# GpSimd's preparation in a two-layer encoder trunk: input matrices ahead of the angle tables, and the first transposes of h one product later

## The chip, the cores and the metric

The kernel runs on one core of one Trainium2 chip. The metric is device time in microseconds (us), the median of repeated executions. Engines go by these names: TensorE (PE; its weight loads are PEld), VectorE (DVE), ScalarE (ACT), GpSimd (POOL) and SyncE (SP).

## What is computed

Two layers over 256 tokens of 1024 channels, all in float32. Each layer is a feed-forward stage (FFN 1), a mixer, and a second feed-forward stage (FFN 2), each with a residual and a layer norm:

```
x <- LN(alpha*x + 0.5*SwiGLU_1(x))
x <- LN(alpha*x + HybridMixer(x))
x <- LN(alpha*x + 0.5*SwiGLU_2(x))

def swiglu_ffn(x, w_up, w_down):            # w_up 1024 x 5632, w_down 2816 x 1024
    gate, up = jnp.split(x @ w_up, 2, axis=-1)
    return (jax.nn.silu(gate) * up) @ w_down

# ssm_branch, 32 groups of 16 channels, 64 complex states each
    a_bar = jnp.exp(lam * dt)
    b_bar = ((a_bar - 1.0) / lam)[:, :, None] * lax.complex(b_re, b_im)
    bu = einsum(u, b_bar)
    states = associative_scan(a_seq, bu)
    y = einsum(states, c_mat).real + d_skip * u
```

The mixer has a state-space branch (above), and a branch of sparse attention with an additive position bias. The state-space branch needs, per layer, matrices that depend on the weights alone: `b_bar`, a product of the output matrix with powers of `a_bar`, and tables of cosine and sine of the angles that turn the scan into a real one. The change is about when GpSimd makes these.

## The kernel before, in words

**The main stream.** TensorE multiplies in float32 by splitting each operand in a high part (rounded to the matmul's format) and a low part, the rest: three matmuls for each product (lines 744 to 746). SyncE loads weight tiles of 128 x 1024 into a ring of four buffers (`raw`, loads at line 329). ScalarE writes the high part into `whi` (`split_hi`, line 430), VectorE the low part into `wlo` (`split_lo`, line 1246); both are rings of eight. A tile's load waits until the tile four before it is split; a split waits until TensorE has used the tile eight before it.

**An FFN** has 11 chunks of 256 hidden channels. `up_chunk` takes the four weight tiles of a chunk twice, once for each half t of the tokens (t = 0, 1), 24 matmuls of 512 columns each (`up_pass`). ScalarE then makes `silu` (line 453), VectorE the product h (line 1274), and TensorE transposes h (`h_transpose`, line 768) for the down product, which ScalarE and VectorE again split (lines 444 and 1264). Chunks 0 to 2 are written out (`PEEL`), the other eight are a hardware loop. In FFN 1 of layer 0 (f = 0) chunk 0 and 1 are written out in `opening`. Then come 22 tiles of the down product. After its tiles 2, 6, 11 and in the last part, TensorE does a quarter of the state-space preparation (`prepare_quarter`, lines 923 to 929): it transposes the four 128 x 128 matrices of `b_bar`, which ScalarE copies to `b_t` (line 468), and multiplies `b_bar` with `c_t`.

**The order in `silu` and h.** On ScalarE and on VectorE the four splits for the chunk two ahead stand between the silu (or h) of t = 0 and that of t = 1. An engine runs its instructions in program order.

**GpSimd** runs `prepare(l)`: for layer 0 during FFN 1 of layer 0, for layer 1 during FFN 2 of layer 0. In order:

- transfers of the parameters (line 1696) and of a column `d_col`; for layer 0 the table of attention biases (`gather_bias`, line 1681, 31 small operations, and its store);
- a wait for VectorE's `clamp` (line 1355), which stands behind chunk 0's h; then the angles, whose sine and cosine ScalarE takes (line 464, behind chunk 1);
- squares, powers and quotients of 128 x 16 (`small`), transfers of the raw input and output matrices `b_raw` and `c_t`, 512 KB each (lines 1752, 1753);
- the tables `tab_c`, `tab_s` by doubling, 7 steps with up to 128 x 512 elements, with `b_bar` as scratch. Between two steps the factor is squared, and copied by two multiplications by one;
- for each quarter q of four: `prepare_b(q)`, 12 operations of 128 x 128, then 6 for `c_t`. There is one `b_bar` buffer, so that `prepare_b(q + 1)` waits until TensorE has used quarter q.

Nearly all of these go through one helper (line 1647), and each waits for the one before it.

```
            def prepare_b(q):
                js = slice(4 * q, 4 * q + 4)
                if q > 0:
                    pool.wait_ge(S["bt_done"], NQ * l + q)
                    pool.wait_ge(S["k0_done"], NQ * l + q)
```

VectorE flips the sign of half of `c_t` (`negate_c`, line 1361) behind the first split of the down product. It needs `c_t` to have landed, and GpSimd's products of `c_t` need it.

Of the kernel before, what the change touches and what calls it, by code (L numbers as in the profile page):

```python
# [13 lines left out]
P = 128  # L14
# [87 lines left out]
def build(nc, A, out):  # L102
# [19 lines left out]
    b_t = sb("b_t", [P, 4, NQ, P])  # L122
# [45 lines left out]
    b_bar = place("b_bar", [P, 4, P])  # L168
# [151 lines left out]
    with block:  # L320
# [102 lines left out]
        def _(act):  # L423
# [23 lines left out]
            def up_chunk(i, f, s, c, b, first=False):  # L447
                for t in range(NT):
# [6 lines left out]
                    if t == 0:  # L455
                        for q in range(4):
                            split_hi(i, s + RING + q)
# [8 lines left out]
            def prepare_b(l, q):  # L466
                act.wait_ge(S["bt_done"], NQ * l + q + 1)
                nc.scalar.copy(b_t[:, :, q, :], ps[:, 0, :].rearrange("p (v n) -> p v n", v=4)
                               ).then_inc(S["bt_ready"], 1)
# [271 lines left out]
        def _(pe):  # L741
# [51 lines left out]
            def up_chunk(i, f, s, c, b):  # L793
                for t in range(NT):
                    up_pass(i, f, s, c, b, t)

            def opening():
# [45 lines left out]
                h_transpose(0, 0, 0, False)  # L843
# [68 lines left out]
            def prepare_quarter(l, f, q):  # L912
# [9 lines left out]
                for v in range(4):  # L922
                    ins = nc.tensor.transpose(ps[:, 0, v * P:v * P + P], b_bar[:, v, :], ident[:, :])
                ins.then_inc(S["bt_done"], 1)
                for r in range(4):
                    o = ps[32 * r:32 * r + 32, 1, 256:288]
                    j = 4 * q + r
                    nc.tensor.matmul(o, b_bar[:, 0, 32 * r:32 * r + 32], c_t[:, 0, j, :], start=True, stop=False)
                    ins = nc.tensor.matmul(o, b_bar[:, 1, 32 * r:32 * r + 32], c_t[:, 1, j, :],
# [3 lines left out]
            def ffn(f, stage, s0, following, prep):  # L933
# [4 lines left out]
                for c in range(2, PEEL):  # L938
                    up_chunk(0, f, s0 + 4 * c, c, c % 2)
# [31 lines left out]
            def ssm_in(l, half):  # L971
# [7 lines left out]
                for q in (2 * half, 2 * half + 1):  # L979
                    u = u_t[:, q, :].rearrange("p (c e) -> p c e", e=2)  # L980
                    for v in range(2):
                        at = (q % 2) * SEQ + v * HALF
                        for e in range(2):
                            for r in range(4):
                                rows = slice(32 * r, 32 * r + 32)
                                ins = nc.tensor.matmul(ps[:, BU + r, at:at + HALF],  # L986
                                                       b_t[rows, 2 + v if e == 0 else v, q, :], u[rows, :, e],
# [241 lines left out]
        def _(dve):  # L1229
# [37 lines left out]
            def up_chunk(i, f, s, c, b, first=False, early=False):  # L1267
                for t in range(NT):
# [8 lines left out]
                    if t == 0:  # L1277
# [93 lines left out]
            def ffn(f, s0, prep):  # L1371
                for c in range(PEEL):
                    up_chunk(0, f, s0 + 4 * c, c, c % 2, first=c == 0, early=c < 2)
                    if c == 0 and prep is not None:
                        clamp(prep)
# [3 lines left out]
                for k in range(HK - RING):  # L1379
# [3 lines left out]
                    if k == 0 and prep is not None:  # L1383
                        negate_c(prep)
# [253 lines left out]
        def _(pool):  # L1638
# [48 lines left out]
            def prepare(l):  # L1687
# [10 lines left out]
                if l == 0:  # L1698
                    gather_bias()
# [16 lines left out]
                op(m(5), m(4), k(12), ALU.add, S["angle_ready"])  # L1716
                pool.wait_ge(S["sincos_ready"], l + 1)
                si, co, mag = m(6), m(7), m(10)

# [32 lines left out]
                pool.dma_start(b_raw[:, :, :, :], A["ssm_b_rows"][l]).then_inc(S["b_landed"], 16)  # L1752
                pool.dma_start(c_t[:, 0:2, :, :], A["ssm_c_rows"][l]).then_inc(S["c_landed"], 16)

                n = 1
# [188 lines left out]
```

## Time and profile before

| what | value |
| --- | --- |
| median of three runs | 1118.56 us (1118.28 to 1119.14) |
| span of the profiled execution, first to last instruction | 1117.5 us |
| what the median has beyond that span | 1.06 us |
| busy: TensorE / its weight loads | 1105.8 us (99%) / 917.9 us (82%) |
| busy: VectorE / ScalarE / GpSimd | 752.0 us (67%) / 561.1 us (50%) / 391.1 us (35%) |
| DMA | 208.95 MB, mean 187 GB/s |

The profile is one execution, read out by hardware. For the profiled execution no time but its span is given; the runs' times include a little before the first and after the last instruction. A row of the order of time has: start in us, duration in us, engine, line, operation, output <- inputs, count, and in brackets the idle time of the engine before it and what ended it. TensorE's matmuls overlap: what counts is the distance from one start to the next, not the duration.

### The profile page before, as it was taken

Reading aid. Unit: us, or ns where it says so; the run is one execution under the profiler, and the core shown is the slowest. Engines: PE = TensorE matmul, PEld = TensorE weight load, DVE = VectorE, ACT = ScalarE, POOL = GpSimd, SP = SyncE. Lnnn points to the kernel's source line nnn. Section 1 sums busy time; section 2 is a strip of 40 time slices with the busy share of each in tenths; the row PEclk is TensorE's granted clock in tenths of the full one; section 3 lists DMA queues with packets and bytes.
Section 4 is the critical chain, followed back from the end, with each engine's and each line's share of the span. In section 5 each row is a group of like instructions: output and inputs, shape, how many; then the busy total and the mean of one; then the engine's idle time right before and its main releaser. Section 6 shows DMA issues by size and latency. Waiting matters only on the chain.

```text
span 1117.5 us, 17726 instructions
## 1 busy us (share of the span) xinstructions
PE 1105.8 (99%) x5979; PEld 917.9 (82%) x5979; DVE 752.0 (67%) x1073; ACT 561.1 (50%) x805; POOL 391.1 (35%) x560
## 2 busy tenths in 40 slices
PE   9999999999999999999999999999999999999997
PEld 7788888997788888888888888889877888888886
DVE  6657755789977865675575555467898787565544
ACT  6545433674873554543344544336748645453540
POOL 4889975107700188998500000011275000000001
PEclk9999999999999999999999999999999999999999
DMA  9776753644565577565367575536535666657541
GB/s 287 242 228 208 247 176 113 211 136 137 157 223 192 166 224 242 184 221 187 112 201 227 159 245 192 192 91 226 164 112 160 209 199 210 211 172 241 189 150 38
DMA packets 158655, 208.95 MB, mean 187 GB/s; under 512 B 12760, under 2 KB 107128, under 8 KB 158592
## 3 DMA queue, kind: packets, MB, share of 16 engines
q1 hardware_dynamic: 155232, 202.29, 56.7%
q10 hardware_dynamic: 2592, 3.67, 1.2%
q0 software_dynamic: 768, 2.17, 0.6%
q8 instruction: 37, 0.61, 0.2%
q14 instruction: 26, 0.21, 0.1%
HBM read 207.02 MB, written 1.06 MB: 186 GB/s over the span
## 4 chain that ended last, share of the span: by engine, by line
PE 82%; DVE 8%; ACT 3%; issue 3%; DMA 2%; SPq 1%; POOLq 0%; POOL 0%; DVEq 0%; ACTq 0%
PE ps L744 25%; PE ps L746 25%; PE ps L745 25%; DVE wlo L1246 4%; PE ps L768 2%; DMA raw<-in_ffn_w_up 1%; DVE score L1441 1%; ACT whi L430 1%; DMA raw<-in_w_in 1%; PE ps L758 1%; PE ps L986 1%; DVE gates L1413 1%; PE ps L1123 1%; PE ps L1125 1%; PE ps L1126 1%
## 5 line engine op out<-in xcount | busy, mean ns | idle before, releaser
L1246 DVE TENSOR_TENSOR wlo<-raw,whi 128x1024 fp32r<-128x1024 f32 (+1 forms) x371 | 475.7, 1298 | 188.4 <-ACT whi L430 174.2
L430 ACT CAST whi<-raw 128x1024 fp32r<-128x1024 f32 (+1 forms) x371 | 384.7, 1044 | 287.1 <-PE ps L746 225.2
L744 PE MATMUL ps<-whi,xh 128*128 128x512 f32 x976 | 384.4, 394 | 0.2 <-DVE wlo L1246 0.2
L746 PE MATMUL ps<-whi,xl 128*128 128x512 f32 x976 | 377.8, 387 | 0.0
L745 PE MATMUL ps<-wlo,xh 128*128 128x512 f32 x976 | 377.4, 387 | 0.0
L744 PEld LDWEIGHTS ps<-whi,xh 128*128 128x128 f32 x976 | 183.3, 188 | 39.0 <-issue 3.4
L746 PEld LDWEIGHTS ps<-whi,xl 128*128 128x128 f32 x976 | 183.2, 188 | 37.8
L745 PEld LDWEIGHTS ps<-wlo,xh 128*128 128x128 f32 x976 | 183.5, 188 | 34.9
L1671 POOL TENSOR_TENSOR rstd<-var_eps,cst 128x1 f32<-128x1 f32 x12 | 18.2, 1518 | 529.8 <-DVE var_eps L1295 520.7
L744 PE MATMUL ps<-whi,hh 128*128 128x512 f32 (+1 forms) x355 | 139.5, 393 | 0.0
L746 PE MATMUL ps<-whi,hl 128*128 128x512 f32 (+1 forms) x355 | 137.7, 388 | 0.0
L745 PE MATMUL ps<-wlo,hh 128*128 128x512 f32 (+1 forms) x355 | 137.6, 388 | 0.0
L1274 DVE SCALAR_TENSOR_TENSOR h<-silu,ps 128x256 f32<-128x256 f32 x88 | 36.4, 416 | 97.6 <-ACT silu L453 97.6
L453 ACT ACTIVATE silu<-ps 128x256 f32<-128x256 f32 x88 | 33.0, 379 | 134.9 <-PE ps L746 134.8
L746 PEld LDWEIGHTS ps<-whi,hl 128*128 128x128 f32 x355 | 66.7, 188 | 13.9
L744 PEld LDWEIGHTS ps<-whi,hh 128*128 128x128 f32 x355 | 66.7, 188 | 13.5
L745 PEld LDWEIGHTS ps<-wlo,hh 128*128 128x128 f32 x355 | 66.7, 188 | 13.1
L1840 POOL TENSOR_TENSOR h_st<-tab_c,gates 128x512 f32<-128x512 f32 x8 | 10.3, 1294 | 115.3 <-DVE wlo L1246 88.6
L1647 POOL TENSOR_TENSOR small<-small 128x16 f32<-128x16 f32 x102 | 38.2, 375 | 8.5 <-ACT small L464 0.7
L1123 PE MATMUL ps<-xh,whi 128*128 128x256 f32 x128 | 37.4, 292 | 0.0
L1125 PE MATMUL ps<-xl,whi 128*128 128x256 f32 x128 | 36.2, 283 | 0.0
L1126 PE MATMUL ps<-xh,wlo 128*128 128x256 f32 x128 | 36.1, 282 | 0.0
(195 smaller groups left out, 1209.3 us busy)
## 6 DMA issues: line engine op xcount, KB each, us to landing
raw<-in_ffn_w_up SPq DMA_DIRECT2D x351, 256.0 KB, 4.0
raw<-in_ffn_w_down SPq DMA_DIRECT2D x176, 256.0 KB, 3.1
raw<-in_w_in SPq DMA_DIRECT2D x128, 256.0 KB, 3.4
raw<-in_w_branch SPq DMA_DIRECT2D x32, 256.0 KB, 3.3
raw<-in_w_out SPq DMA_DIRECT2D x32, 256.0 KB, 3.8
bias_g<-bias_rows ACTq DMA_DIRECT2D x16, 192.0 KB, 3.7
raw<-in_w_in SPq DMA_DIRECT2D x16, 148.0 KB, 2.3
affine<-in_ln_g SPq DMA_DIRECT2D x4, 512.0 KB, 5.6
```

Source lines behind the costliest of these rows:

```text
L430: nc.scalar.copy(whi[:, s % RING, 0:w], raw[:, s % RAW, 0:w]).then_inc(S["hi_done"], 1)
L453: nc.scalar.activation(silu[:, t, :], ps[:, 2 * b + t, 0:CW], ACT.Silu).then_inc(S["silu_done"], 1)
L744: nc.tensor.matmul(o, ah, bh, start=start, stop=False)
L745: nc.tensor.matmul(o, ah, bl, start=False, stop=False)
L746: return nc.tensor.matmul(o, al, bh, start=False, stop=stop)
L768: ins = nc.tensor.transpose(ps[:, 4 + b, k * SEQ + i * P:k * SEQ + (i + 1) * P], h[:, b, i, k * P:(k + 1) * P], ident[:, :])
L1123: nc.tensor.matmul(o, hi, xh[:, k, :], start=k == 0 and m % 2 == 0, stop=False, skip_group_check=True)
L1125: nc.tensor.matmul(o, hi, xl[:, k, :], start=False, stop=False, skip_group_check=True)
L1126: ins = nc.tensor.matmul(o, lo, xh[:, k, :], start=False, stop=k == KT - 1, skip_group_check=True)
L1246: nc.vector.tensor_tensor(wlo[:, s % RING, 0:w], raw[:, s % RAW, 0:w], f32(whi[:, s % RING, 0:w]), ALU.subtract).then_inc(S["split_done"], 1)
L1274: nc.vector.scalar_tensor_tensor(out=h[:, b, t, :], in0=silu[:, t, :], scalar=0.5, in1=ps[:, 2 * b + t, CW:2 * CW], op0=ALU.mult, op1=ALU. ...
L1647: ins = nc.gpsimd.tensor_tensor(o, a, b, f)
```

## The change

It does five things.

1. GpSimd's order in `prepare`: the bias table runs after the angles, while ScalarE takes sine and cosine; the transfers of `b_raw` and `c_t` are issued ahead of it. After the powers come `prepare_b(0)`, `prepare_b(1)` and all four products of `c_t`, then the tables, then `prepare_b(2)` and `prepare_b(3)`.
2. `b_bar` has two buffers (q % 2), so that only quarters 2 and 3 wait for TensorE. The tables use the last quarter of `b_t` as scratch, and `b_t` is laid out quarter by quarter.
3. The copies by multiplication by one between table steps are gone: two pairs of `small` rows change places.
4. VectorE runs `clamp` ahead of chunk 0 and `negate_c` behind chunk 2. `clamp` waits for the parameters' landing.
5. In FFN 1 of layer 0, chunk 0, silu and h of t = 1 run ahead of the four splits on ScalarE and VectorE; and TensorE transposes chunk 0's h not ahead of chunk 2 but inside its first pass, after two of the four tiles.

```
-                    if t == 0:
+                    if t == (1 if f == 0 and first else 0):
                         for q in range(4):
                             split_hi(i, s + RING + q)
...
                 up_pass(0, 0, 4, 1, 1, 1, False)
-                h_transpose(0, 0, 0, False)
...
                 for c in range(2, PEEL):
-                    up_chunk(0, f, s0 + 4 * c, c, c % 2)
+                    first_turn = (lambda: h_transpose(0, 0, 0, False)) if f == 0 and c == 2 else None
+                    up_chunk(0, f, s0 + 4 * c, c, c % 2, first_turn)
                     h_transpose(f, c - 1, (c - 1) % 2, False)
...
             def ffn(f, s0, prep):
+                if prep is not None:
+                    clamp(prep)
                 for c in range(PEEL):
                     up_chunk(0, f, s0 + 4 * c, c, c % 2, first=c == 0, early=c < 2)
-                    if c == 0 and prep is not None:
-                        clamp(prep)
+                if prep is not None:
+                    negate_c(prep)
...
-                if l == 0:
-                    gather_bias()
                 pool.wait_ge(S["par_landed"], 16 * (l + 1))
...
                 op(m(5), m(4), k(12), ALU.add, S["angle_ready"])
+                pool.dma_start(b_raw[:, :, :, :], A["ssm_b_rows"][l]).then_inc(S["b_landed"], 16)
+                pool.dma_start(c_t[:, 0:2, :, :], A["ssm_c_rows"][l]).then_inc(S["c_landed"], 16)
+                if l == 0:
+                    gather_bias()
                 pool.wait_ge(S["sincos_ready"], l + 1)
...
+                    if q >= 2:
+                        pool.wait_ge(S["bt_done"], NQ * l + q - 1)
+                        pool.wait_ge(S["k0_done"], NQ * l + q - 1)
...
+                pool.wait_ge(S["b_landed"], 16 * (l + 1))
+                pool.wait_ge(S["ct_ready"], l + 1)
+                prepare_b(0)
+                prepare_b(1)
+                for q in range(NQ):
+                    js = slice(4 * q, 4 * q + 4)
+                    cmul(c_t[:, 2, js, :], c_t[:, 3, js, :], col(11, js), col(12, js), c_t[:, 0, js, :],
+                         c_t[:, 1, js, :], -1, S["ca_ready"])
...
-                        square(m(21), m(22), m(18), m(19))
-                        op(m(18), m(21), k(14), ALU.mult)
-                        op(m(19), m(22), k(14), ALU.mult)
+                        square(m(then[0]), m(then[1]), m(now[0]), m(now[1]))
+                        now, then = then, now
+                prepare_b(2)
+                prepare_b(3)
```

VectorE's `up_chunk` has the same change of condition around `split_lo`.

The first place is VectorE's order at the opening of FFN 1 of layer 0. `small<-params` is the clamp, `h<-silu,ps` the product h, `wlo` the splits; the semaphores in brackets are what a row waits for. Before:

```order
L1623 CAST ident_bf<-ident 128x128 [waits ident_landed]
L1274 SCALAR_TENSOR_TENSOR h<-silu,ps 128x256 [waits silu_done,const_ready]
L1246 TENSOR_TENSOR wlo<-raw,whi 128x1024 [waits hi_done] x4
L1274 SCALAR_TENSOR_TENSOR h<-silu,ps 128x256 [waits silu_done]
L1355 TENSOR_SCALAR small<-params 128x16 [waits par_landed]
```

and with the change:

```order
L1623 CAST ident_bf<-ident 128x128 [waits ident_landed]
L1355 TENSOR_SCALAR small<-params 128x16 [waits par_landed,const_ready]
L1274 SCALAR_TENSOR_TENSOR h<-silu,ps 128x256 [waits silu_done] x2
L1246 TENSOR_TENSOR wlo<-raw,whi 128x1024 [waits hi_done] x4
L1274 SCALAR_TENSOR_TENSOR h<-silu,ps 128x256 [waits silu_done]
```

The clamp has moved ahead of both h of chunk 0, and these ahead of the four splits.

The second place is GpSimd's order where the powers end and the first quarter or the tables begin. Before:

```order
L1647 TENSOR_TENSOR tab_s<-tab_c 128x16
L1752 DMA b_raw<-in_ssm_b_rows 128x1024
L1753 DMA c_t<-in_ssm_c_rows 128x1024
L1766 TENSOR_TENSOR tab_c<-tab_c,small 128x16
L1647 TENSOR_TENSOR b_bar<-tab_s,small 128x16
```

and with the change:

```order
L1647 TENSOR_TENSOR tab_s<-tab_c 128x16
L1726 TENSOR_TENSOR b_bar<-small,b_raw 128x128
L1647 TENSOR_TENSOR tmp<-small,b_raw 128x128
L1647 TENSOR_TENSOR b_bar<-b_bar,tmp 128x128
L1729 TENSOR_TENSOR b_bar<-small,b_raw 128x128
```

The first table step has given place to the first quarter of `b_bar`; the two transfers stand earlier, behind the angles.

## Rows read from the trace of the kernel before

**Rows 1.** The page, busy time of each engine, share of the span, instructions

```profile
PE 1105.8 (99%) x5979; PEld 917.9 (82%) x5979; DVE 752.0 (67%) x1073; ACT 561.1 (50%) x805; POOL 391.1 (35%) x560
```

**Rows 2.** Waits of TensorE: who for whom, us in total, times, longest

```profile
PE ps L768 <- DVE h L1274: 0.7, 1, 0.7
```

**Rows 3.** Order of time on TensorE, end of chunk 1: start, duration, line

```profile
28.26 0.39 PE L745 MATMUL ps<-wlo,xh 128*128 128x512 f32 x1
28.48 0.39 PE L746 MATMUL ps<-whi,xl 128*128 128x512 f32 x1
29.53 0.66 PE L768 MATMUL ps<-ident,h 128*128 128x128 f32 x4 [0.65 <-DVE h L1274]
29.94 0.47 PE L744 MATMUL ps<-whi,xh 128*128 128x512 f32 x1
```

**Rows 4.** Order of time on ScalarE, chunk 0 and 1

```profile
21.76 0.38 ACT L453 ACTIVATE silu<-ps 128x256 f32<-128x256 f32 x1
...
26.83 1.05 ACT L430 CAST whi<-raw 128x1024 fp32r<-128x1024 f32 x1 [1.37 <-DMA raw<-in_ffn_w_up]
```

**Rows 5.** Order of time on VectorE, the same stretch

```profile
22.26 0.42 DVE L1274 SCALAR_TENSOR_TENSOR h<-silu,ps 128x256 f32<-128x256 f32 x1 [0.39 <-ACT silu L453]
...
27.91 1.23 DVE L1246 TENSOR_TENSOR wlo<-raw,whi 128x1024 fp32r<-128x1024 f32 x1 [1.07 <-ACT whi L430]
29.06 0.41 DVE L1274 SCALAR_TENSOR_TENSOR h<-silu,ps 128x256 f32<-128x256 f32 x1
```

**Rows 6.** Order of time on TensorE, end of chunk 2

```profile
40.95 0.60 PE L768 MATMUL ps<-ident,h 128*128 128x128 f32 x4
41.30 0.48 PE L744 MATMUL ps<-whi,xh 128*128 128x512 f32 x1
```

**Rows 7.** Stretches of GpSimd: length, busy us (operations), TensorE's clock, DMA share, GB/s

```profile
12.96:24.37 11.41, 11.11 (x32) 1.00 0.96 298
29.71:40.21 10.50, 9.40 (x15) 1.00 0.94 298
40.55:58.89 18.34, 15.83 (x33) 1.00 0.73 227
60.38:128.97 68.59, 62.87 (x90) 1.00 0.71 229
129.04:139.20 10.16, 9.60 (x12) 1.00 0.65 208
141.59:149.84 8.25, 7.70 (x12) 1.00 0.56 190
176.83:182.25 5.42, 4.87 (x12) 1.00 0.32 97
```

**Rows 8.** Operations of GpSimd by form, 60.3 to 129 us: busy, mean ns

```profile
L1647 POOL TENSOR_TENSOR small<-small,cst 128x16 f32<-128x16 f32 x18 | 8.8, 492 | 1.4
```

**Rows 9.** Order of time on TensorE, the third quarter

```profile
167.39 0.60 PE L923 MATMUL ps<-ident,b_bar 128*128 128x128 f32 x4
```

**Rows 10.** Order of time on VectorE, two bursts of four splits

```profile
41.71 4.68 DVE L1246 TENSOR_TENSOR wlo<-raw,whi 128x1024 fp32r<-128x1024 f32 x4 [0.52 <-ACT whi L430]
...
94.98 8.04 DVE L1246 TENSOR_TENSOR wlo<-raw,whi 128x1024 fp32r<-128x1024 f32 x4 [1.42 <-ACT whi L430]
```

**Rows 11.** FFN 2 of layer 0: line 1696's transfers, then GpSimd, VectorE, TensorE, GpSimd

```profile
DMA to landing us min/median/max: 3.6/4.4/5.3
...
393.01 2.93 POOL L1647 TENSOR_TENSOR small<-cst,params 128x16 f32<-128x16 f32 x1 [8.17 <-DVE small L1355]
...
387.14 5.30 DVE L1246 TENSOR_TENSOR wlo<-raw,whi 128x1024 fp32r<-128x1024 f32 x4 [2.44 <-ACT whi L430]
...
395.33 0.60 PE L768 MATMUL ps<-ident,h 128*128 128x128 f32 x4
...
534.24 0.40 POOL L1782 TENSOR_TENSOR b_bar<-small,b_raw 128x128 f32<-128x128 f32 x1 [2.68 <-PE ps L929]
```

**Rows 12.** TensorE in the last 7.4 us: busy (matmuls), granted clock, DMA share, GB/s

```profile
1110.00:1117.40 7.40, 0.29 (x3) 0.84 0.19 71
```

More of the change, by code:

```diff
@@ L121, in build @@
     y_h, y_l, ys_h, ys_l = y_hl[:, 0], y_hl[:, 1], ys_hl[:, 0], ys_hl[:, 1]
-    b_t = sb("b_t", [P, 4, NQ, P])
+    b_t = sb("b_t", [P, NQ, 4, P])
     c_t = sb("c_t", [P, 4, NJ, 32])
@@ L167, in build @@
     b_raw = place("b_raw", [P, 2, NJ, 32])
-    b_bar = place("b_bar", [P, 4, P])
+    b_bar = place("b_bar", [P, 2, 4, P])
     tmp = place("tmp", [P, P])
@@ L467, in prepare_b @@
                 act.wait_ge(S["bt_done"], NQ * l + q + 1)
-                nc.scalar.copy(b_t[:, :, q, :], ps[:, 0, :].rearrange("p (v n) -> p v n", v=4)
+                nc.scalar.copy(b_t[:, q, :, :], ps[:, 0, :].rearrange("p (v n) -> p v n", v=4)
                                ).then_inc(S["bt_ready"], 1)
@@ L791, in up_pass, with up_chunk @@
                     ins.then_inc(S["up_done"], 1)
-            def up_chunk(i, f, s, c, b):
+            def up_chunk(i, f, s, c, b, between=None):
                 for t in range(NT):
-                    up_pass(i, f, s, c, b, t)
+                    up_pass(i, f, s, c, b, t, True, between if t == 0 else None)
             def opening():
@@ L922, in prepare_quarter @@
                 for v in range(4):
[L923 removed]
+                    ins = nc.tensor.transpose(ps[:, 0, v * P:v * P + P], b_bar[:, q % 2, v, :], ident[:, :])
                 ins.then_inc(S["bt_done"], 1)
@@ L927, in prepare_quarter @@
                     j = 4 * q + r
-                    nc.tensor.matmul(o, b_bar[:, 0, 32 * r:32 * r + 32], c_t[:, 0, j, :], start=True, stop=False)
-                    ins = nc.tensor.matmul(o, b_bar[:, 1, 32 * r:32 * r + 32], c_t[:, 1, j, :],
+                    nc.tensor.matmul(o, b_bar[:, q % 2, 0, 32 * r:32 * r + 32], c_t[:, 0, j, :], start=True, stop=False)
+                    ins = nc.tensor.matmul(o, b_bar[:, q % 2, 1, 32 * r:32 * r + 32], c_t[:, 1, j, :],
                                            start=False, stop=True)
@@ L986, in ssm_in @@
                                 ins = nc.tensor.matmul(ps[:, BU + r, at:at + HALF],
-                                                       b_t[rows, 2 + v if e == 0 else v, q, :], u[rows, :, e],
+                                                       b_t[rows, q, 2 + v if e == 0 else v, :], u[rows, :, e],
                                                        start=e == 0, stop=e == 1)
@@ L1276, in up_chunk @@
                                                    op1=ALU.mult).then_inc(S["h_ready"], 1)
-                    if t == 0:
+                    if t == (1 if f == 0 and first else 0):
                         for q in range(4):
@@ L1759, in prepare @@
                         js = slice(j, j + step)
-                        pr = m(18)[:, js].unsqueeze(2).to_broadcast([P, step, n])
-                        pi = m(19)[:, js].unsqueeze(2).to_broadcast([P, step, n])
-                        t = b_bar[:, :, :].rearrange("p v n -> p (v n)")[:, 0:step * n].rearrange(
+                        pr = m(now[0])[:, js].unsqueeze(2).to_broadcast([P, step, n])
+                        pi = m(now[1])[:, js].unsqueeze(2).to_broadcast([P, step, n])
+                        t = b_t[:, NQ - 1, :, :].rearrange("p v n -> p (v n)")[:, 0:step * n].rearrange(
                             "p (j n) -> p j n", j=step)
```

53 lines of the change are left out of this document (19 added, 34 removed).

## The prediction, made before the changed kernel ran

> **What bounds the kernel now.** I read the page's busy shares first: TensorE is busy for 1105.8 of the 1117.5 us of the span [rows 1], so 11.7 us is all that removed waits could give, start and tail included. The waits of TensorE come next [rows 2]. In the two feed-forward stages (FFNs) that prepare the state-space matrices there is one: 0.7 us, once, at the transposes of h (line 768). The third view is the order of time around that one wait [rows 3]: the last matmul of chunk 1 starts at 28.48 us, 0.22 after the one before it, the four transposes at 29.53, the next matmul at 29.94. Chunk 2's 48 matmuls lie between 29.94 and the next transposes at 40.95 [rows 6], 0.23 us each, so 28.71 is where work should have gone on. Line 923, the transposes of `b_bar`, does not appear among TensorE's waits at all. The step that GpSimd's reordering serves is today on time.
>
> Why h is late is seen on two engines. ScalarE makes silu of token half 0 at 21.76 us, then four splits, the last of which waits for its weight tile and runs at 26.83, and only then silu of half 1 [rows 4]. VectorE does its h of half 0 at 22.26, the last split from 27.91 on, and h of half 1 from 29.06 to 29.47 [rows 5]. TensorE finished chunk 0 before it began chunk 1, so a product whose inputs had long been there waits behind a weight transfer.
>
> **Term 1, the opening: -0.87 us.** The silu of half 1 now follows at once. It would end near 22.4 us, its h by about 23.0. Nothing that TensorE needs for the first product of chunk 2 is then outstanding, so that pass can start at 28.71. The transposes run after its second weight tile. There they still cost something: in the stream they start at 40.95 and the next matmul at 41.30 [rows 6], that is 0.35 us against 0.41 at the opening. The gain is 29.53 - 28.71 = 0.82 plus 0.06, taken as 0.87. Bounds: 0 if another wait takes its place, 0.9 if all of it goes.
>
> What is late next? The first three splits of chunk 2 move by about 0.3 us, a silu and an h. The last does not: it waits for its transfer and still runs at 27.91 [rows 5], ending near 29.1, and TensorE needs it only after three tiles and the transposes, near 33.2. The splits of chunk 3 come up to 0.3 us later; they begin behind the h of 29.06, and TensorE takes that chunk up at 41.30 [rows 6], so 12 us stand against four splits of 1.2 to 2.0 us and transfers of about 4. That costs nothing.
>
> **Term 2, GpSimd's order, FFN 1 of layer 0: 0, in 0 to +8.2.** The clamp runs ahead of the first h, so GpSimd starts its chain at about 22.2 instead of 29.7. I add its stretches from [rows 7]: angles 10.5; two DMA issues 1.2 (they leave their later place); the bias table 11.4, which ran before inside the wait for the clamp and now stands in the chain; powers 18.3. That is 63.6. Then two quarters of `b_bar`. A quarter took 10.16 where splits came in a burst and 8.25 where they came singly, so I take 9.2 each, 82.0. The four products of `c_t` took 5.42 for two in the quiet end; I take 12.4, in 10.8 to 14.1, which gives 94.4. The tables took 68.59. Twelve small multiplications by one leave them: 18 of that form were busy 8.8 us [rows 8], 0.57 each with the gap, so 6.8 us less, giving 156.2. The third quarter adds 8.3, which gives **164.5**. TensorE asks for it at 167.39 [rows 9], 0.87 earlier after term 1, **166.5**. That is a margin of 2 us on a sum of 142 us. Its ends: quarters -1.9/+1.9, `c_t` -1.6/+1.7, removed operations down to 0.30 us each, +3.2, last quarter +1.9, early stretches +-1.5: from about 160 to 175 when all go one way. The likelier result is no wait; the upper bound is a wait of 8.2 us. Nor can it be a gain, since TensorE does not wait there today.
>
> That stretch is loose because a GpSimd operation's duration hangs on where VectorE's splits fall. Two rows show it: four splits took 4.68 us with small GpSimd operations beside them and 8.04 beside operations of 512 columns [rows 10], and the same 12 operations of a quarter took 8.25 or 10.16. The Trainium skill, "SBUF — State Buffer", section "Who interferes with whom", says that a VectorE instruction with two SBUF inputs and a GpSimd one that reads SBUF shut each other out for the whole instruction, and that issue order decides who blocks. By that rule the sum isn't a sum of fixed prices, it locks onto the splits' rhythm; it is a reason to give the late third quarter more chance than my margin alone would, and the trace agrees.
>
> The cover of the tables on VectorE: in the second half of the FFN they run beside one split per weight tile, and a tile takes TensorE 12 matmuls, 2.7 us. A split drawn out to 8.04/4 = 2.0 us still fits. Cost 0; if it did not fit, eight ring slots would still have to be used up first.
>
> The fourth quarter would be ready 8.3 us after the third. TensorE asks for it two full weight tiles and five half ones later, 54 matmuls or 12.4 us. Nothing there.
>
> **Term 3, FFN 2 of layer 0, which prepares layer 1: 0.** There is no bias table. GpSimd's first operation waited 8.17 us for the clamp and started at 393.01; its two DMA issues (1.2 us) stand before that wait, so the parameters' transfer was issued near 383.7, and such transfers landed in 3.6 to 5.3 us [rows 11]. VectorE now waits for it before its first h, until 387.3 to 389.0. Queued behind this wait are h of chunk 0 and the four splits for chunk 2, which began at 387.14 and took 5.30; they would end at 394.9 at worst. TensorE is done with chunk 1 when it transposes at 395.33 [rows 11], takes up chunk 2 then, and needs the fourth split 4 us after. Free, by a small margin. GpSimd's chain starts 4 to 5 us sooner and has no bias table in it: 388.5 plus 130.9 is 519.4. In the profile the third quarter's products ended just before 534.24 [rows 11]. The margin is 13.
>
> **Edits at nothing.** The new layout of `b_t` lets ScalarE's copy write 512 columns in a row instead of four pieces; it runs in idle time of ScalarE. The two input DMAs of 512 KB each now fall near 35 us, where transfers are dense; the weights of chunk 3 and 4 have 4 us and more in hand. The sign change of `c_t` makes VectorE wait for that transfer, issued by 36; it stands behind chunk 2's splits, which end past 46 [rows 10], and the slowest parameter transfer took 5.3 us.
>
> **The sum.** -0.87 + 0 + 0 = -0.87 us. The profiled span of 1117.5 would be 1116.6. The median of the three runs is 1118.56, 1.1 above the span, which I carry over since neither the start nor the tail is touched: 1118.56 - 0.87 = **1117.7 us**.
>
> **The rivals.** (A) As above, 1117.7: chance 0.55.
> (B) The third quarter is 0.4 to 3.1 us late for TensorE at layer 0. Against it stands the margin of 2 us, for it the error of a sum of 142. Net -0.5 to +2.2, so 1118.1 to 1120.8: 0.27.
> (C) Slower. The same wait is over 3.1 us, because the bias table in the chain and the tables' 18 large operations fall into bursts of splits. It decides from a third quarter ready after 169.6 on; at the bound of 175 the time is 1118.56 - 0.87 + 8.2 = 1125.9. A waiting TensorE may also lose clock. After its last matmul the granted clock of the last 7.4 us averages 0.84 [rows 12], which is some 2.4 us at 1.2 GHz among 2.4; as long a stretch behind a wait would cost 1.2 us more, as half the work is done in it. Chance of C 0.10. The Trainium skill, "TensorE: Matmul & The Clock Gate", section "What's actually happening", holds the throttled clock for the default that activity lifts. By it a long enough wait would cost more than its length; no run here shows a wait of that kind inside the stream.
> (D) The change does not do what it says at the opening: another input of chunk 2 is late (a split of tile 8 behind two h), and the wait only moves. 1118.6: 0.05.
> (E) Faster by more than 2.2 us. Only 0.9 us of idle lies in the places touched, so this would need something the trace does not show: 0.03.
>
> **How the numbers follow.** A measurement of this kernel tells about 0.2%, 2.2 us, from no change: below 1116.3 is faster, above 1120.8 slower. A, B and D lie between, 0.87; C gives slower 0.10, E faster 0.03. The range reaches from 0.6 us under A (the three runs lie within 0.9) to 1120.0, which takes in D and most of B and leaves out C and E: 1117.1 to 1120.0.
>
> **What would show it.** Right: no wait at line 768 near 29 us; matmuls from 28.5 on 0.23 apart; the transposes of chunk 0 between two weight tiles; `b_bar` of the third quarter written before 166.5 us; all later TensorE work 0.9 us earlier. Wrong: a TensorE wait on `b_bar` near 166 us (B, C), a gap near 28.7 on a split (D), or a VectorE wait at the clamp near 384 us that TensorE feels at 395.

## The result, and the profile after

| | median, us | lowest to highest | runs |
| --- | --- | --- | --- |
| before | 1118.60 | 1118.28 to 1119.14 | 4 |
| changed | 1123.46 | 1122.93 to 1127.34 | 4 |

The ratio of changed to before is 1.0051, with an interval of 1.0038 to 1.0064: slower by 4.9 us, outside the predicted range and on the other side of the forecast. The profiled execution of the changed kernel took 1122.93 us, with a span of 1121.1.

The page of the changed kernel: the busy shares, TensorE's granted clock in 40 slices, and the head of the chain that ended last.

```profile
PE 1107.1 (99%) x5979; PEld 919.5 (82%) x5979; DVE 748.4 (67%) x1073; ACT 561.5 (50%) x805; POOL 388.9 (35%) x536
...
PEclk9999998999999999999999999999999999999999
...
PE 79%; POOL 12%; issue 2%; DVE 2%; ACT 2%; DMA 1%; SPq 0%; POOLq 0%; DVEq 0%; ACTq 0%
```

The busy shares hardly moved [rows 1]. What is new is the digit 8 in a PEclk row that is otherwise 9 (the seventh slice, 168 to 196 us), and 12% of GpSimd in the chain. Before, the chain had none:

```profile
PE 82%; DVE 8%; ACT 3%; issue 3%; DMA 2%; SPq 1%; POOLq 0%; POOL 0%; DVEq 0%; ACTq 0%
```

The waits of TensorE in the changed kernel (who for whom, us in total, times, longest):

```profile
PE ps L922 <- POOL b_bar L1647: 4.3, 1, 4.3
```

The wait at line 768 [rows 2] is gone, and one of 4.3 us on the third quarter of `b_bar` stands in its place. First the opening, where [rows 3] had the transposes behind chunk 1. Order of time on TensorE in the changed kernel (start, duration, line, operation):

```profile
27.84 0.39 PE L746 MATMUL ps<-whi,xl 128*128 128x512 f32 x1
28.07 0.39 PE L744 MATMUL ps<-whi,xh 128*128 128x512 f32 x1
...
30.79 0.60 PE L768 MATMUL ps<-ident,h 128*128 128x128 f32 x4
31.14 0.48 PE L744 MATMUL ps<-whi,xh 128*128 128x512 f32 x1
```

Chunk 1 ends with the matmul of 27.84; chunk 2 goes on 0.23 later; the transposes stand after twelve matmuls, and cost the 0.35 us from 30.79 to 31.14 as in [rows 6]. This part did what it should. Then the third quarter, which answers to [rows 9]:

```profile
165.63 0.39 PE L746 MATMUL ps<-whi,hl 128*128 128x512 f32 x1
170.33 1.12 PE L922 MATMUL ps<-ident,b_bar 128*128 128x128 f32 x4 [4.31 <-POOL b_bar L1647]
...
171.77 0.80 PE L744 MATMUL ps<-whi,hh 128*128 128x512 f32 x1
172.79 0.63 PE L746 MATMUL ps<-whi,hl 128*128 128x512 f32 x1
...
174.50 0.58 PE L744 MATMUL ps<-whi,hh 128*128 128x512 f32 x1
174.91 0.40 PE L745 MATMUL ps<-wlo,hh 128*128 128x512 f32 x1
```

TensorE asked at 165.9 and waited until 170.3. (Here and below, "asked" is the start of the last matmul before plus 0.23 us; the idle time in brackets comes out 0.15 shorter.) After it, matmuls of 512 columns stand 0.43 apart up to 174.50 and 0.23 apart again from 174.91 on. The same stretch in windows (length, TensorE busy and its matmuls, granted clock, DMA share, GB/s):

```profile
165.00:170.00 5.00, 1.02 (x5) 0.81 0.62 195
170.00:175.00 5.00, 4.67 (x28) 0.51 0.24 88
175.00:180.00 5.00, 5.00 (x24) 1.00 0.08 14
```

The granted clock averages 0.51 from 170 to 175: TensorE ran nearly all of it at 1.2 GHz, not 2.4. Its idle time before was the 4.3 us, and the 0.81 of the window ahead says that the clock fell while it waited.

**The budget.** Starts of the same pieces of TensorE's work, in us, in two profiles of the kernel before (the second is the run `r_before_again` below) and two of the changed kernel:

| distance | before | before, again | changed | changed, again | changed - before |
| --- | --- | --- | --- | --- | --- |
| start to second quarter of `b_bar` | 152.84 | 153.46 | 151.31 | 151.26 | -1.53 |
| second to third quarter | 14.55 | 14.55 | 19.02 | 19.08 | +4.47 |
| third to fourth quarter | 13.19 | 13.18 | 15.26 | 14.69 | +2.07 |
| fourth to second group of scores of layer 0 | 104.82 | 104.36 | 103.81 | 104.06 | -1.01 |
| from there to the last matmul | 824.62 | 824.34 | 824.27 | 824.15 | -0.35 |
| last matmul starts at | 1110.02 | 1109.89 | 1113.67 | 1113.24 | +3.65 |

So the loss is two adjoining things, the wait (+4.5) and the matmuls at half the clock behind it (+2.1). The opening gives back 1.5. The row of -1.0 is a wait on ScalarE in attention (line 1038), which was 1.01 us in the first profile, 0.5 in the second and between 0 and 0.8 in the ten others, whatever the kernel; I count it as scatter. The profiles differ by 3.6 us and the medians by 4.9: execution time stands 1.8 to 1.9 us above the span in the changed kernel's four runs, so the profile before (1117.5) lay some 0.7 above its own median, and the one after 0.5 below.

**Where GpSimd's time went.** The chain of the changed kernel in the stretches of term 2, in the form of [rows 7]: angles, bias table, powers, two quarters of `b_bar`, four products of `c_t`, tables, third quarter.

```profile
21.34:36.52 15.18, 14.08 (x15) 1.00 0.91 295
37.70:46.93 9.23, 8.92 (x32) 1.00 0.96 311
46.93:67.40 20.47, 17.96 (x33) 1.00 0.71 221
67.48:81.98 14.50, 13.32 (x24) 1.00 0.57 181
82.06:100.46 18.40, 17.22 (x24) 1.00 0.60 181
100.53:162.10 61.57, 56.77 (x78) 1.00 0.64 219
162.17:170.28 8.11, 7.55 (x12) 0.86 0.65 213
```

### The profile page after: what moved, and what is told of

Its sections match the earlier page's. It is cut to its first block, busy times and chain, and to the rows that moved or that the text cites. A ratio compares the mean times of both kernels' runs of the same rounds, so it can differ in the third digit from the quotient of the medians.

```text
span 1121.1 us, 17692 instructions
## 1 busy us (share of the span) xinstructions
PE 1107.1 (99%) x5979; PEld 919.5 (82%) x5979; DVE 748.4 (67%) x1073; ACT 561.5 (50%) x805; POOL 388.9 (35%) x536
## 3 DMA queue, kind: packets, MB, share of 16 engines
HBM read 207.02 MB, written 1.06 MB: 186 GB/s over the span
## 4 chain that ended last, share of the span: by engine, by line
PE 79%; POOL 12%; issue 2%; DVE 2%; ACT 2%; DMA 1%; SPq 0%; POOLq 0%; DVEq 0%; ACTq 0%
PE ps L744 23%; PE ps L746 23%; PE ps L745 23%; POOL small L1647 4%; PE ps L1123 2%; PE ps L1125 1%; PE ps L1126 1%; PE ps L768 1%; DVE wlo L1246 1%; POOL tmp L1647 1%; POOL b_t L1647 1%; POOL tab_s L1647 1%; DMA raw<-in_ffn_w_up 1%; PE ps L758 1%; POOL bias_sb L1681 1%
## 5 line engine op out<-in xcount | busy, mean ns | idle before, releaser
L1671 POOL TENSOR_TENSOR rstd<-var_eps,cst 128x1 f32<-128x1 f32 x12 | 18.2, 1516 | 553.2 <-DVE var_eps L1295 544.1
L1647 POOL TENSOR_TENSOR small<-small 128x16 f32<-128x16 f32 x102 | 56.9, 558 | 7.9
```

What stands on the lines that cost most here:

```text
L1647: ins = nc.gpsimd.tensor_tensor(o, a, b, f)
L1671: nc.gpsimd.tensor_tensor(rstd[:, i, :], var_eps[:, i, :], cst[:, 0:1], ALU.pow).then_inc(S["rstd_ready"], 1)
```

## The experiments

In short, with the ratio to the kernel before and its interval where several runs were made. The kernel before was run beside them each time: 1119.18 beside `e1` to `e4` (35 runs, 1118.06 to 1121.46), 1118.92 beside `e5` and `r_after_again` (15 runs, 1118.33 to 1120.17).

| run | kernel | median, us (runs) | ratio | third quarter: written, asked |
| --- | --- | --- | --- | --- |
| `r_after_again` | changed, again | 1125.65 (5) | 1.0055 [1.0041, 1.0068] | 170.3, 165.8 |
| `e1_bias_first` | changed, bias table first again | 1117.70 (11) | 0.9984 [0.9975, 0.9993] | 162.6, 166.5 |
| `e2_opening_only` | before + part 5 | 1118.53 (11) | 0.9996 [0.9986, 1.0006] | no wait there |
| `e3_no_opening` | changed without part 5 | 1122.94 (12) | 1.0028 [1.0015, 1.0040] | 171.4, 167.2 |
| `e4_ask_later` | changed, third quarter two tiles later | 1117.75 (11) | 0.9985 [0.9976, 0.9993] | 168.0, 171.7 |
| `e5_open_ask_later` | before + part 5, quarters 1, 2 one tile later | 1117.99 (11) | 0.9990 [0.9981, 0.9999] | no wait there |
| `e6_late_9` | `e1` + 9 idle operations | 1118.74 (1) | | 166.8, 165.8 |
| `e7_late_13` | `e1` + 13 idle operations | 1122.49 (1) | | 169.3, 166.3 |
| `e8_one_input` | changed, low part a copy | 1115.10 (1) | | 146.4, 165.8 |
| `r_before_again` | before, again | 1119.17 (1) | | no wait there |

### `e1_bias_first`: is it the bias table in the chain?

```
+                if l == 0:
+                    gather_bias()
                 pool.wait_ge(S["par_landed"], 16 * (l + 1))
...
-                if l == 0:
-                    gather_bias()
                 pool.wait_ge(S["sincos_ready"], l + 1)
```

> The changed kernel, with the bias table back ahead of the wait for the clamp. Theory 1 (the bias table inside GpSimd's chain makes the third quarter late): 9.2 us leave the chain, 3 us come back because the chain now starts behind the table near 24.4 instead of 21.3; the third quarter is ready near 164, TensorE asks near 165.9 and does not wait; 6.5 us below the changed kernel, near 1117. Rival 2 (the length of the chain is set by collisions with VectorE's splits, and a shift is given back in them): a wait of 1 to 3 us stays, 1119 to 1121.

Measured: 1117.70, no wait at line 922, span 1115.9. GpSimd's table runs from 14.08 to 26.4 with its store until 27.2; the clamp was done at 21.7, so that only the first 7.6 us of it fill the wait. The chain starts at 27.24, and the third quarter is written at 162.6:

```profile
162.11 0.46 POOL L1647 TENSOR_TENSOR b_bar<-b_bar,tmp 128x128 f32<-128x128 f32 x1
```

Putting the 31 small operations back ahead of the clamp takes the whole loss away, and 1.5 us of gain against the runs beside it is left. Part 1's other half, the input matrices ahead of the tables, is harmless. But the table is less than half of the 7.7 us by which the third quarter comes sooner: 9.2 us leave the chain, and its start moves back by 5.9 (21.34 to 27.24), which leaves 3.3. The other 4.4 are stretches that fell elsewhere among the splits (angles 11.4 us and not 15.2, powers 18.5 and not 20.5, products of `c_t` 15.3 and not 18.4, against two quarters at 17.4 and tables at 63.1, which are longer). The 3.3 alone would have put the third quarter at 167.0, 0.5 behind TensorE's question. The expectation had a start at 24.4 and a quarter near 164; that it came close is two misses that largely cancel, a start 2.8 us later and stretches 4.4 us shorter. So the experiment shows that this order has no wait, and not that the table's length was the whole cause.

### `e3_no_opening` and `e2_opening_only`: the two parts alone

```
-                    if t == (1 if f == 0 and first else 0):
+                    if t == 0:
...
+                h_transpose(0, 0, 0, False)
...
-                    first_turn = (lambda: h_transpose(0, 0, 0, False)) if f == 0 and c == 2 else None
+                    first_turn = None
```

> The changed kernel without its edit of the opening. If GpSimd's chain is pinned to the start of the program and TensorE waits for it, what TensorE loses at the opening it waits less at the third quarter: same time as the changed kernel, 1122.5 to 1124. Rival (the two parts add up): 0.9 to 1.5 us slower than it, 1124.4 to 1125.

Measured: 1122.94, but the twelve runs go from 1118.98 to 1125.57, so that in some the loss is almost gone. The profiled one took 1125.05:

```profile
171.45 1.11 PE L923 MATMUL ps<-ident,b_bar 128*128 128x128 f32 x4 [4.13 <-POOL b_bar L1648]
```

The third quarter is written at 171.4 and asked for at 167.2, the matmuls behind it are 0.43 apart for some ten, and the distance from the third to the fourth quarter is 15.93 against 13.19. The reordering loses by itself; the earlier opening did not bring the wait about.

`e2_opening_only` is the kernel before with part 5 alone, the reverse of the diff above:

> The kernel before, with the later transposes and the h of half 1 ahead of the splits alone. All theories: no wait at the first transposes, 0.9 to 1.5 us below the kernel before, 1117.1 to 1117.7. If the 1.5 us that the two profiles show at the opening are partly chance in the first transfers, it is 0.9.

Measured: 1118.53, no difference that can be told; ten runs lie between 1117.73 and 1119.06, and one took 1123.36 at a mean clock of 0.995 where the others have 0.998 or 0.999. No profile shows what that one did. Order of time on TensorE at the first quarter in this kernel:

```profile
138.75 0.39 PE L746 MATMUL ps<-whi,hl 128*128 128x512 f32 x1
140.57 0.66 PE L922 MATMUL ps<-ident,b_bar 128*128 128x128 f32 x4 [1.43 <-POOL b_bar L1647]
```

The gain of the opening (its transposes of h at the end of chunk 2 stand at 39.45 us where [rows 6] have 40.95) is handed back at the first quarter. Before, that quarter was written at 139.2 ([rows 7], the stretch that ends there) and its transposes stood at 140.51: a margin of 1.3 us. Here TensorE asks at 139.0, and GpSimd, in the same order, writes it at 140.5, because its powers ended at 62.0 where [rows 7] have 58.89. So the sooner question took up the margin, and the wait itself is the longer chain; whether that comes from the opening or is one execution's, a single profile doesn't tell: the other two profiles of this order of GpSimd's have the quarter at 139.8 (`r_before_again`) and 140.5 (`e5_open_ask_later`). In this profile, then, the opening gains nothing without GpSimd's new order or a later question.

### `e4_ask_later` and `e5_open_ask_later`: ask where the answer is ready

```
-PREP = {2: 0, 6: 1, 11: 2}
+PREP = {2: 0, 6: 1, 13: 2}
```

> The changed kernel with TensorE's third quarter asked for after down tile 13 instead of 11, 5.5 us later, near 171.3. Ready was 170.3, so the wait of 4.3 us goes, and with it the 2 us at the lower clock behind it: 6.5 us below the changed kernel, near 1117. If the slower clock were not caused by the wait, only 4.3 us come back, 1119.

Measured: 1117.75, no wait, span 1115.2. With the third quarter asked for at 171.7 the changed kernel keeps its gain. Ahead of that quarter nothing differs from the changed kernel, yet it is written at 168.0 and not 170.3: the chain scatters by some 2 us between executions. `e5_open_ask_later` does the same for the old order, on `e2_opening_only`, with `{3: 0, 7: 1, 11: 2}`:

> The kernel before, with the edit of the opening, and TensorE asking for the first two quarters after down tiles 3 and 7 instead of 2 and 6. GpSimd's order is the old one. The opening alone had -1.5 us at 41 us and gave it back in a wait of 1.4 us for the first quarter at 139. Theory (given back because GpSimd's chain is pinned to the start): the wait goes, the gain stays, 0.8 to 1.5 us below the opening alone, 1117.1 to 1117.8. Rival (the opening is worth only 0.9, the rest is chance of transfers): 1118.0 to 1118.5.

Measured: 1117.99, no wait, span 1116.2. Three kernels (`e1`, `e4`, `e5`) end within 0.3 us of one another and below the kernel before, by 0.16, 0.15 and 0.10%. All three have the opening and no wait on `b_bar`. `e1` and `e4` have the lowest medians of those that compute everything. For `e5` the wait went as expected; its worth is less clear, since 1117.99 lies between the theory's 1117.8 and the rival's 1118.0, and its interval overlaps that of `e2_opening_only`.

### `e6_late_9` and `e7_late_13`: what a wait costs beyond its length

Both are `e1_bias_first` with operations ahead of the third quarter whose result nobody reads:

```
+                if l == 0:
+                    for _ in range(13):
+                        op(m(20), m(18), m(19), ALU.mult)
                 prepare_b(2)
```

> The variant with the bias table first, whose third quarter was ready at 162.6 with TensorE asking at 166.5, with 9 idle multiplications of GpSimd (0.3 to 0.6 us each) ahead of the third quarter in layer 0. Ready 165.3 to 168: a wait of 0 to 1.5 us. If the clock falls only behind longer waits, TensorE goes on at full clock and the time is that of the variant plus the wait, 1117.7 to 1119.2.

> The same with 13 idle multiplications. Ready 166.5 to 170: a wait of 0 to 3.5 us. Theory (the lower clock follows a wait of this length too): matmuls start every 0.43 us for some us behind it and the time grows by more than the wait. Rival (it takes the 4.1 us and more of the changed kernel): the time grows by the wait alone.

Order of time on TensorE, nine operations:

```profile
165.53 0.39 PE L746 MATMUL ps<-whi,hl 128*128 128x512 f32 x1
166.80 0.66 PE L922 MATMUL ps<-ident,b_bar 128*128 128x128 f32 x4 [0.88 <-POOL b_bar L1647]
...
168.24 0.40 PE L746 MATMUL ps<-whi,hl 128*128 128x512 f32 x1
168.47 0.40 PE L744 MATMUL ps<-whi,hh 128*128 128x512 f32 x1
```

and thirteen:

```profile
166.06 0.39 PE L746 MATMUL ps<-whi,hl 128*128 128x512 f32 x1
169.33 0.66 PE L922 MATMUL ps<-ident,b_bar 128*128 128x128 f32 x4 [2.87 <-POOL b_bar L1647]
...
170.77 0.58 PE L746 MATMUL ps<-whi,hl 128*128 128x512 f32 x1
171.14 0.63 PE L744 MATMUL ps<-whi,hh 128*128 128x512 f32 x1
...
173.70 0.63 PE L744 MATMUL ps<-whi,hh 128*128 128x512 f32 x1
174.13 0.44 PE L745 MATMUL ps<-wlo,hh 128*128 128x512 f32 x1
174.41 0.39 PE L746 MATMUL ps<-whi,hl 128*128 128x512 f32 x1
```

Behind a wait of 0.88 us the matmuls are 0.23 apart as ever. Behind one of 2.87 the clock holds for 1.4 us more, and then, from 170.77 to 174.41, nine matmuls stand up to 0.43 apart. From third to fourth quarter the two take 13.26 and 14.85 us, against 13.18 in `e1_bias_first`: 0.1 and 1.7 us beyond the wait's own length. Both are single runs: the 3.75 us in time between them go with 2.0 us more wait and 1.6 of slower matmuls.

### `e8_one_input`: is it VectorE that holds GpSimd up?

The low part is a copy of the raw weights here and the subtraction is left out, so that what this kernel computes is no longer the product.

```
-                nc.vector.tensor_tensor(wlo[:, s % RING, 0:w], raw[:, s % RAW, 0:w],
-                                        f32(whi[:, s % RING, 0:w]), ALU.subtract
-                                        ).then_inc(S["split_done"], 1)
+                nc.vector.tensor_copy(wlo[:, s % RING, 0:w], raw[:, s % RAW, 0:w]
+                                      ).then_inc(S["split_done"], 1)
```

> The changed kernel, but VectorE's low part of each split is a plain copy of the raw weights: one SBUF input in place of two (the subtraction is left out). In the changed kernel the four products of c_t took 18.4 us beside such splits (their operations 617 to 811 ns each, where the kernel before had 399 and 459 beside no split), a split's low part 1.34 us at the mean, and the third quarter of layer 0 came at 170.3. Theory (GpSimd and VectorE hold each other up only where VectorE reads two SBUF inputs): the c_t operations fall to 0.40 to 0.46 us, the four products to some 11 us, the copies take 0.4 to 0.7 us each, the third quarter is ready before 163, TensorE does not wait at line 922 and the time is 1117.0 to 1118.0. Rival (any VectorE instruction of that size on SBUF holds GpSimd up, whatever its inputs, or the chain is long for reasons of its own): the c_t operations keep over 0.6 us, the third quarter comes at 165 to 171 and TensorE waits up to 4 us.

Measured: 1115.10, no wait at line 922. Two of the stretches of GpSimd, the angles and the products of `c_t`; all are in a table in the next section:

```profile
21.07:31.91 10.84, 9.74 (x16) 1.00 0.94 297
...
68.65:81.31 12.66, 11.48 (x24) 1.00 0.56 171
```

Groups of GpSimd's operations on `c_t` (busy us, mean ns, idle), the changed kernel:

```profile
L1647 POOL TENSOR_TENSOR c_t<-c_t,tmp 128x128 f32<-128x128 f32 x8 | 6.5, 811 | 0.6
L1647 POOL TENSOR_TENSOR tmp<-small,c_t 128x128 f32<-128x128 f32 x8 | 6.1, 767 | 0.0
```

and `e8_one_input`:

```profile
L1646 POOL TENSOR_TENSOR c_t<-c_t,tmp 128x128 f32<-128x128 f32 x8 | 4.6, 575 | 0.6
L1646 POOL TENSOR_TENSOR tmp<-small,c_t 128x128 f32<-128x128 f32 x8 | 3.7, 457 | 0.0
```

The operation that came at 767 ns beside the subtraction comes at 457 beside the copy. The `c_t` products take 12.7 us, not the 11 expected, but every stretch is shorter, the sum by 33.8 us of 147.5, and the third quarter is there at 146.4, after 10.0 us of waiting for the buffer that TensorE gives back. So what VectorE runs sets the length of GpSimd's chain. The condition in the theory, two SBUF inputs, is not borne out: the copy has one, and holds GpSimd up too. Order of time on VectorE and on GpSimd, `e8_one_input`:

```profile
72.08 0.69 DVE L1246 CAST wlo<-raw 128x1024 fp32r<-128x1024 f32 x1 [0.66 <-ACT whi L430]
...
72.16 0.86 POOL L1646 TENSOR_TENSOR tmp<-small,c_t 128x128 f32<-128x128 f32 x1
...
75.74 0.68 DVE L1263 TENSOR_TENSOR hl<-ps,hh 128x512 f32 x1
...
75.89 0.40 POOL L1725 TENSOR_TENSOR c_t<-small,c_t 128x128 f32<-128x128 f32 x1
```

Counted over the first 200 us, 14 of 78 GpSimd operations of 128 x 128 take more than 0.55 us here, all beside a copy, and 16 of 78 in the changed kernel, all beside a split. So about as many are held, each for less, as the copy is shorter (0.69 us at the median against 1.23). `hl`, as long as a copy but with one of its inputs in PSUM, holds up none in either kernel where it runs alone beside them. Nor is it any VectorE instruction, then; what the copy and the subtraction have and `hl` lacks, no run here tells. The time also lies 2.6 us below `e4_ask_later`, mostly late in the kernel (from the second group of scores to the last matmul 823.1 us, in `e1_bias_first` 824.7), which was not followed up.

### `r_after_again` and `r_before_again`: what differs from one execution to the next

> The changed kernel once more, for its spread. Theory 1 (TensorE waits for the third quarter, and the length of GpSimd's chain moves by some us from run to run as its operations meet VectorE's splits): a median of 1121 to 1124 and a spread of 4 us or more, against 1.3 us in the variant with the bias table first; a wait at line 922 of 2 to 6 us in the profile. Rival (a fixed delay): a spread of 1 us like the others.

Measured: five runs from 1122.54 to 1126.33, a spread of 3.8 us against 1.3 in `e1_bias_first`, and a median of 1125.65, above the 1121 to 1124 expected. The profiled one has the wait again at 4.4 us, and fewer slow matmuls behind it (14.69 from third to fourth quarter, first run 15.26).

> The kernel before, unchanged, for a second profile of it. If the 0.35 us that the opening gained beyond the forecast lay in a wait of the one profile (a split of chunk 1 at 21.8 us), this profile has its transposes of h earlier than 29.5 us; if it belongs to the kernel, they stand at 29.5 again. The same for TensorE's wait of 1.01 us in attention at 277 to 286 us: there again, or between 0 and 0.8 us as in the other profiles.

Measured: 1119.17, span 1117.4. The opening in this profile, on TensorE:

```profile
30.14 0.33 PE L768 MATMUL ps<-ident,h 128*128 128x128 f32 x1 [1.32 <-DVE h L1274]
```

Neither of the two expectations: the wait is not gone but twice as long, 1.32 us where [rows 3] have 0.65, because the last weight tile of the four came to ScalarE at 27.44 and not at 26.83 [rows 4]. The opening's wait scatters with the transfers, so the gain is 1.5 us against the one profile and 2.1 against the other. The wait in attention was 0.5 us, between the others.

## Why the prediction was wrong

The number failed in one term, term 2; the mechanism that decided was the one named as rival C, at a chance of 0.10.

**What bounds it; the place.** Right. TensorE is at 99% in both, and the only thing that mattered was the margin of the third quarter at layer 0, "2 us on a sum of 142".

**Term 1, the opening: right in sign and place, too small.** Forecast -0.87, came as -1.53. The wait at line 768 and its transposes gave what was summed. The rest is 0.6 us of scatter in when TensorE gets to chunk 1's end (27.84 against 28.48), which rests on the landing of weight tiles and was not in the sum. The prediction also read one wait in this stage where there were two: TensorE waited 0.20 us for a split at 21.78 in the profile before. And the term may not stand alone: in its profile `e2_opening_only` hands it back at the first quarter, whose margin of 1.3 us the prediction had not read. Rival D, that another input of chunk 2 is late, did not occur.

**Term 2, GpSimd's chain: the step that failed.** Its parts, forecast and measured:

| stretch | forecast | changed | `e1_bias_first` | `e8_one_input` |
| --- | --- | --- | --- | --- |
| start of the chain, us | 22.2 | 21.3 | 27.2 | 21.1 |
| angles | 10.5 | 15.2 | 11.4 | 10.8 |
| two DMA issues | 1.2 | 1.2 | 1.2 | 1.4 |
| bias table | 11.4 | 9.2 | ahead of the chain | 7.6 |
| powers | 18.3 | 20.5 | 18.5 | 14.9 |
| two quarters of `b_bar` | 18.4 | 14.5 | 17.4 | 12.7 |
| four products of `c_t` | 12.4 | 18.4 | 15.3 | 12.7 |
| tables | 61.8 | 61.6 | 63.1 | 48.7 |
| third quarter | 8.3 | 8.1 | 8.2 | 6.3 |
| third quarter ready, us | 164.5 | 170.3 | 162.6 | 146.4, with 10.0 of waiting |

The largest single miss is the `c_t` term: 12.4, bounded at 14.1, and it was 18.4 (14.6 to 18.4 in the seven profiles of this order with the subtraction). The price was read from two products in the quiet end [rows 7], where operations take 0.40 and 0.46 us, with some allowance for splits. In the new place two bursts of four splits stood beside them. Order of time on VectorE, then on GpSimd, in the changed kernel:

```profile
82.08 5.54 DVE L1246 TENSOR_TENSOR wlo<-raw,whi 128x1024 fp32r<-128x1024 f32 x4 [1.53 <-ACT whi L430]
87.87 0.68 DVE L1264 TENSOR_TENSOR hl<-ps,hh 128x512 f32 x1
93.45 5.31 DVE L1246 TENSOR_TENSOR wlo<-raw,whi 128x1024 fp32r<-128x1024 f32 x4 [1.42 <-ACT whi L430]
...
82.42 1.38 POOL L1647 TENSOR_TENSOR tmp<-small,c_t 128x128 f32<-128x128 f32 x1
...
87.96 0.47 POOL L1647 TENSOR_TENSOR c_t<-c_t,tmp 128x128 f32<-128x128 f32 x1
```

Operations of this form take 1.26 to 1.54 us beside a split and 0.40 or 0.46 free of one; `hl` adds nothing. The two quarters ahead of them met one burst and took 14.5, less than their 18.4. The pair trades: together 32.9 against 30.8 forecast, and 32 to 33 us in all seven profiles. So the largest miss net of that trade is the angles, +4.7: 10.5 was read at 29.7 to 40.2, beside four splits, and from 21.3 on they meet eight, the four of the opening and the four behind. The rows show a multiplication of 128 x 16 there at 1.09 and 1.15 us where it takes 0.22 undisturbed, the first of them here with the split beside it:

```profile
29.20 1.23 DVE L1246 TENSOR_TENSOR wlo<-raw,whi 128x1024 fp32r<-128x1024 f32 x1
...
29.41 1.09 POOL L1647 TENSOR_TENSOR small<-params,small 128x16 f32<-128x16 f32 x1
```

The powers add 2.2, the tables without their twelve small operations came out as forecast, and the bias table (-2.2) and the earlier start (-0.9) cost less. The total missed by 5.8 us, because the terms were treated as fixed prices that err independently, while each depends on how many splits it meets. The two profiles of the changed kernel show how such a chain falls in with the splits: the bias table ended at 46.9 us in one and 45.7 in the other, and from 128.9 us on the two chains stand at the same times, to the third quarter at 170.3.

A VectorE instruction with two SBUF inputs and a GpSimd one that shut each other out, the later issued waiting for the whole of the other, would make such a rhythm; that is the rule that the prediction cited from the Trainium skill, "SBUF — State Buffer", section "Who interferes with whom". The rows above agree, 1.38 us beside a subtraction with two SBUF inputs and 0.47 beside `hl`, which has one. `e8_one_input` does not test it, since its copy with one input held GpSimd up as well. The prediction had cited the rule as a reason to give a late third quarter more chance, and gave 0.37 in all, with 0.10 to the case that came.

**What the wait cost.** Rival C priced the length and 1.2 us of clock, from the last 7.4 us [rows 12]. The length came as its rule has it, ready less asked, 170.3 less 165.9. The clock was 2.1 us and not 1.2, since the work behind the wait ran at half the clock for longer; the two profiles of the changed kernel, `e7_late_13` and `e3_no_opening` give 2.1, 1.5, 1.7 and 2.7 more from third to fourth quarter than before. With the measured 170.3 in place of its 164.5, the prediction's own sum under C is 1118.56 - 0.87 + 3.8 + 1.2 = 1122.7, against 1123.46. The other page that the prediction cited from the Trainium skill, "TensorE: Matmul & The Clock Gate", section "What's actually happening", has the throttled clock as the default, from which the prediction worked out that a long enough wait would cost more than its length. The trace agrees: the rows at 0.43 us show it inside the stream, which no row of before could.

**The tables' cover and the fourth quarter.** Right: TensorE waits at no split there, and the fourth quarter was written 5.5 us after the third and not waited for.

**Term 3, FFN 2 of layer 0: right.** VectorE's rows in the changed kernel, all 4.0 us later than before by the loss above:

```profile
391.29 0.17 DVE L1355 TENSOR_SCALAR small<-params 128x16 f32<-128x16 f32 x1 [3.88 <-DMA params<-in_ssm_params]
...
391.70 4.80 DVE L1246 TENSOR_TENSOR wlo<-raw,whi 128x1024 fp32r<-128x1024 f32 x4
```

The clamp waits for the parameters until 391.29, which is 387.3 less the shift, the lower end of the forecast. The four splits end at 396.5, and TensorE transposes at 399.4. The third quarter of layer 1 is written at 531.9 and asked for at 537.1: a margin of 5 us where 13 was forecast. The `c_t` products took 18.2 us there too, so the same term erred the same way, with room. Less the shift of 4.0, the third quarter came 8.5 us after the forecast 519.4, and the margin took it.

**What stood above the span.** 1.06 us was carried over; where span and time are shown for one execution of either kernel it is 1.8 to 1.9. It moves both kernels alike.

**Still open.** Executions of the changed kernel spread over 4.8 us (1122.5 to 1127.3), those of `e1` over 1.3 and those of the kernel before over 3.4. The mean clock of the longest, 0.995, is also that of one of the shortest (1122.93), so it isn't only the clock, and neither profile of this kernel was one of the long ones. How much of the wait each edit of GpSimd's order brings, apart from the splits that its operations happen to meet, isn't shown either.

## What to carry to other kernels

Don't price a moved chain of small GpSimd operations in the place it leaves: give each operation the price that rows show beside what will run there, count the splits that it will meet, and read the margin of every later question, the first as well as the last. Work that fills a wait costs nothing where it stands; moved into the chain it costs its length (9.2 us here), less what it would have delayed the start of the chain where it stood (5.9), and both against a margin of 2. And in this stream a wait of TensorE of some 3 us or more cost its length and 1.5 to 2.7 us on top.

## What the runs showed of the hardware

- A wait of 0.9 us in the stream left the granted clock at 2.4 GHz, and one of 2.9 us was followed by some nine matmuls at 1.2 GHz, beginning only 1.4 us after work had resumed; behind 4.3 us the lower clock was there at once. The cost beyond the wait was 0.1 us after 0.9, 1.7 after 2.9, and 1.5 to 2.7 after 4.1 to 4.4.
- A GpSimd multiplication of 128 x 16 took 0.22 us alone and up to 1.15 beside a VectorE subtraction of 128 x 1024 with two SBUF inputs; one of 128 x 128 took 0.40 and 1.38. A VectorE copy of 128 x 1024, with one SBUF input and 0.69 us long, also held GpSimd up, to 0.86 us; `hl`, 0.68 us long with one input in PSUM and one in SBUF, did not.
- The same 24 operations on `c_t` took from 14.6 us (both kernels with idle operations) to 18.4 in kernels that differ in when they start among the splits, and a chain that was 1.2 us ahead had lost all of it 80 us later.
